# Every second pair of gate and side tiles of a ConvFFN made with seven half-size products instead of eight

## The chip, the cores and the metric

The kernel runs on one core of one Trainium2 chip. The metric is the device time of one execution in microseconds (us). TensorE multiplies, VectorE and ScalarE work on tiles in SBUF and PSUM, SyncE issues the loads of weights.

## What is computed

Two layers of a streaming encoder work on 512 tokens of 1024 features in float32. Layer 0 has a Mamba-2 mixer, layer 1 a short gated convolution; each is followed by a gated ConvFFN, and RMSNorms stand before and after each block. The change lies in the ConvFFN alone:

```python
FFN_HIDDEN = 2816
FFN_CONV_W = 3

def conv_ffn(h, w_up, conv_w, conv_b, w_down):
    up = h @ w_up
    gate = causal_dwconv(up[..., :FFN_HIDDEN], conv_w, conv_b)
    val = up[..., FFN_HIDDEN:]
    return (jax.nn.silu(gate) * val) @ w_down

x = x + rms_norm(f, ffn_post_g[i])        # f is what conv_ffn gives, for each layer i
```

## The kernel before

Activations are held with features on the 128 partitions and the 512 tokens in a row. A float32 product is made of three passes of TensorE: every operand is split in a high part (a copy in the type fp32r, made by ScalarE) and a low part (original minus high part, made by VectorE), and `three` multiplies high by high, low by high and high by low. A **unit** is one 1024x128 column strip of a weight matrix. SyncE loads it into one of two raw buffers (`w_raw`), ScalarE writes `w_hi` (`splits_to` there, L362), VectorE writes `w_lo` (`splits_to` there, L592), each into one of five slots, and TensorE runs it in `unit`: eight feature tiles by three passes, 24 matmuls of 128x128 by 128x512 (L863 to L865) into one PSUM bank. The first two units of each stage are run as two halves of 256 tokens each (`half_unit`, 24 matmuls of 256 columns each), since they start while the norm before them is being finished.

The up stage of a layer takes the 22 hidden tiles t = 0 to 21 one after the other. Each has a gate unit and a side unit, in turn. Around them stands a fixed order of work, written by hand in `ffn_up`, once for ScalarE and once for VectorE:

- VectorE scales the gate bank by the norm's row into `cpad` (L807), makes the low part of a later unit (L592), adds the two early taps of the convolution (L794, twice), scales the side bank into `side` (L811), makes another low part (L592), multiplies gate by side into `gated` (L816), and makes the low part of that product, `hid_lo` (L799).
- ScalarE starts the convolution in `acc` (L549), makes a high part of a unit (L362), takes the SiLU (L553), makes another high part (L362), and makes `hid_hi` (L556).

All instructions of an engine run in the order written. The down stage (`project`) multiplies `hid_hi` and `hid_lo` with 22 units of the down matrix; every unit takes 24 matmuls of 512 columns. `enter` covers the joint of two stages, `boundary` is what ScalarE and VectorE do there. Semaphores order the engines: `w_lo_done` (a unit is ready), `unit_done` (a bank is complete), `gate_in` and `side_in` (a bank is free again).

Of the kernel before, what the change touches and what calls it, by code (L numbers as in the profile page):

```python
# [10 lines left out]
P = 128  # L11
# [4 lines left out]
def build(nc, x, mix_pre_g, mix_post_g, ffn_pre_g, ffn_post_g, ssd_w_in, ssd_conv_w, ssd_conv_b,  # L16
# [129 lines left out]
    SC_BANKS = (2, 3, 4, 5, 6, 7)  # L146
    AHEAD = 2
# [5 lines left out]
    with ctx:  # L153
# [27 lines left out]
        x_sums, r_pre_tok = col(3, C), col(3, C)  # L181
# [33 lines left out]
        with ExitStack() as rest:  # L215
# [10 lines left out]
            acc, gated, side = (sb(n, [P, T], stack=rest) for n in ("acc", "gated", "side"))  # L226
            hid_hi, hid_lo = sb("hid_hi", [P, FT, T], F32R, rest), sb("hid_lo", [P, FT, T], F32R, rest)
# [120 lines left out]
        def _(act):  # L348
# [3 lines left out]
            def splits_to(end):  # L352

                for u in range(split_at[0], min(end, U_END)):
                    act.wait_ge(raw_landed[u % 2], 16 * (u // 2 + 1))
                    if before(u) is not None:
                        act.wait_ge(unit_done, before(u) + 1)
                    elif u == U_OUT + 3:
# [117 lines left out]

            def post_sum(b, c, half):
                if 2 * c + half < 7:
                    act.wait_ge(proj_done, 7 * b.nth + 2 * c + half + 1)
                else:  # L480
                    act.wait_ge(unit_done, b.end)
# [33 lines left out]
            def boundary(b, first):  # L515
# [25 lines left out]
                nc.scalar.activation(r_pre_tok[:, b.nth, :], x_sums[:, b.nth, :], ACT.Sqrt, bias=eps[:], scale=1.0 / D).then_inc(pre_root, 1)  # L541
                splits_to(b.end + AHEAD + 2)
# [3 lines left out]
            def ffn_up(layer, t):  # L546
                u, n = U_UP[layer] + 2 * t, HID0[2 * layer] + t
                act.wait_ge(gate_in, n + 1)
                nc.scalar.activation(acc[:], cpad[:, CW - 1:CW - 1 + T], ACT.Identity, bias=one(col_ffn_b(layer, t)),  # L549
                                     scale=one(col_ffn_w(layer, CW - 1, t))).then_inc(acc_done, 1)  # L550
                splits_to(u + 4)
                act.wait_ge(tap_done, 2 * n + 2)
                nc.scalar.activation(acc[:], acc[:], ACT.Silu).then_inc(act_done, 1)  # L553
                splits_to(u + 5)
                act.wait_ge(gated_done, n + 1)
                nc.scalar.activation(hid_hi[:, t, :], gated[:], ACT.Copy).then_inc(hid_hi_done, 1)  # L556

            def sc_in(i):
# [6 lines left out]
                nc.scalar.activation(hid_hi[:, i, :], gated[:], ACT.Copy).then_inc(hid_hi_done, 1)  # L565
# [6 lines left out]
            for t in range(FT):  # L572
                ffn_up(0, t)
# [5 lines left out]
            for t in range(FT):  # L579
                ffn_up(1, t)  # L580
# [4 lines left out]
        def _(dve):  # L585
            split_at = [1]

            def splits_to(end):

                for u in range(split_at[0], min(end, U_END)):  # L590
                    dve.wait_ge(w_hi_done, u + 1)
                    nc.vector.tensor_tensor(w_lo[slot(u)][:], w_raw[:, u % 2, :], w_hi[slot(u)][:].bitcast(F32),  # L592
# [204 lines left out]
            def low_hidden(n, t):  # L797
                dve.wait_ge(hid_hi_done, n + 1)
                nc.vector.tensor_tensor(hid_lo[:, t, :], gated[:], hid_hi[:, t, :].bitcast(F32), ALU.subtract).then_inc(hid_lo_done, 1)  # L799

            sides = [0]

            def ffn_up(layer, t):
                u, n = U_UP[layer] + 2 * t, HID0[2 * layer] + t
                banks = [UP_BANKS[layer][2 * (t % 2) + half] for half in range(2)]
                dve.wait_ge(unit_done, u + 1)
                nc.vector.tensor_tensor(cpad[:, CW - 1:CW - 1 + T], bank[banks[0]][:], r_row[:, 0, :], ALU.mult).then_inc(gate_in, 1)  # L807
                splits_to(u + 4)
                taps(n, lambda tap: col_ffn_w(layer, tap, t))
                dve.wait_ge(unit_done, u + 2)  # L810
                nc.vector.tensor_tensor(side[:], bank[banks[1]][:], r_row[:, 0, :], ALU.mult).then_inc(side_in, 1)  # L811
                sides[0] += 1
                splits_to(u + 5)
                dve.wait_ge(side_in, sides[0])
# [356 lines left out]
```

## Time and profile before

| | |
|---|---|
| median of 3 runs | 1339.2 us (1339.18 to 1339.48) |
| time of the profiled execution | 1340.12 us |
| its span from the first to the last instruction | 1338.4 us |
| TensorE busy in it | 1327.8 us, 99% |
| VectorE busy | 786.2 us, 59% |
| ScalarE busy | 570.9 us, 43% |
| mean granted clock of TensorE | 0.999 |

The busy time of an engine is the time in which at least one of its instructions ran. Matmuls overlap in the pipeline, so the rate of TensorE is read from the starts of matmuls that follow each other and not from their lengths. Instructions of VectorE and ScalarE overlap too, by a little under 0.1 us, where the second doesn't wait for anything.

### The profile page before, as it was taken

Reading aid. Unit: us, or ns where it says so; the run is one execution under the profiler, and the core shown is the slowest. Engines: PE = TensorE matmul, PEld = TensorE weight load, DVE = VectorE, ACT = ScalarE, POOL = GpSimd, SP = SyncE. Lnnn points to the kernel's source line nnn. Section 1 sums busy time; section 2 is a strip of 40 time slices with the busy share of each in tenths; the row PEclk is TensorE's granted clock in tenths of the full one; section 3 lists DMA queues with packets and bytes.
Section 4 is the critical chain, followed back from the end, with each engine's and each line's share of the span. In section 5 each row is a group of like instructions: output and inputs, shape, how many; then the busy total and the mean of one; then the engine's idle time right before and its main releaser. Section 6 shows DMA issues by size and latency. Waiting matters only on the chain.

```text
span 1338.4 us, 15750 instructions
## 1 busy us (share of the span) xinstructions
PE 1327.8 (99%) x6382; PEld 1109.5 (83%) x6382; DVE 786.2 (59%) x1140; ACT 570.9 (43%) x875; POOL 28.1 (2%) x30
## 2 busy tenths in 40 slices
PE   8999999999999999999999999999999999999998
PEld 6888888888888888888888888888888888888886
DVE  5888888888526666556632265445566666564223
ACT  6766665556315533333331262223554333333112
POOL 1000000000000000000000000000000000000000
PEclk9999999999999999999999999999999999999999
DMA  5533233442331333333343313334233333334331
GB/s 155 158 110 110 80 97 109 125 121 69 128 108 48 95 107 98 95 95 95 95 137 115 95 32 112 102 102 126 63 88 102 95 97 101 102 96 126 97 109 63
DMA packets 181772, 135.68 MB, mean 101 GB/s; under 512 B 5645, under 2 KB 169893, under 8 KB 180677
## 3 DMA queue, kind: packets, MB, share of 16 engines
q1 hardware_dynamic: 181653, 134.62, 33.5%
q8 instruction: 50, 0.82, 0.3%
q14 instruction: 21, 0.17, 0.0%
q10 hardware_dynamic: 48, 0.07, 0.0%
HBM read 132.51 MB, written 2.16 MB: 101 GB/s over the span
## 4 chain that ended last, share of the span: by engine, by line
PE 98%; ACT 1%; DMA 1%; DVE 0%; issue 0%; SPq 0%; DVEq 0%; ACTq 0%
PE bank L863 22%; PE bank L864 22%; PE bank L865 22%; PE bank L926 9%; PE bank L928 9%; PE bank L927 9%; PE bank L1065 1%; PE bank L1075 1%; PE bank L903 1%; PE bank L1055 1%; DMA x_tok<-in_x 1%; PE bank L1048 1%; PE bank L1040 0%; PE bank L1043 0%; PE bank L1001 0%; ACT mask L423 0%
## 5 line engine op out<-in xcount | busy, mean ns | idle before, releaser
L863 PE MATMUL bank<-h_hi,w_hi 128*128 128x512 f32 (+1 forms) x1328 | 509.0, 383 | 0.0
L865 PE MATMUL bank<-h_lo,w_hi 128*128 128x512 f32 (+1 forms) x1328 | 506.7, 382 | 0.0
L864 PE MATMUL bank<-h_hi,w_lo 128*128 128x512 f32 (+1 forms) x1328 | 506.5, 381 | 0.0
L592 DVE TENSOR_TENSOR w_lo<-w_raw,w_hi 128x1024 fp32r<-128x1024 f32 x227 | 285.1, 1258 | 324.2 <-ACT w_hi L362 324.2
L362 ACT ACTIVATE w_hi<-w_raw 128x1024 fp32r<-128x1024 f32 x227 | 237.1, 1051 | 196.3 <-PE bank L928 172.5
L865 PEld LDWEIGHTS bank<-h_lo,w_hi 128*128 128x128 f32 x1328 | 249.5, 188 | 48.2
L863 PEld LDWEIGHTS bank<-h_hi,w_hi 128*128 128x128 f32 x1328 | 249.6, 188 | 48.0
L864 PEld LDWEIGHTS bank<-h_hi,w_lo 128*128 128x128 f32 x1328 | 249.7, 188 | 47.6
L926 PE MATMUL bank<-w_hi,hid_hi 128*128 128x512 f32 x416 | 162.4, 390 | 0.0
L928 PE MATMUL bank<-w_hi,hid_lo 128*128 128x512 f32 x416 | 161.9, 389 | 0.0
L927 PE MATMUL bank<-w_lo,hid_hi 128*128 128x512 f32 x416 | 161.8, 389 | 0.0
L928 PEld LDWEIGHTS bank<-w_hi,hid_lo 128*128 128x128 f32 x416 | 78.1, 188 | 16.3
L926 PEld LDWEIGHTS bank<-w_hi,hid_hi 128*128 128x128 f32 x416 | 78.1, 188 | 16.0
L927 PEld LDWEIGHTS bank<-w_lo,hid_hi 128*128 128x128 f32 x416 | 78.1, 188 | 15.9
L794 DVE SCALAR_TENSOR_TENSOR acc<-cpad,par,acc 128x512 f32<-128x512 f32 x104 | 77.9, 749 | 3.6 <-ACT acc L549 1.8
L621 DVE SCALAR_TENSOR_TENSOR feat<-pad,par,feat 128x512 f32<-128x512 f32 x96 | 71.5, 751 | 13.7 <-ACT feat L397 11.4
L553 ACT ACTIVATE acc<-acc 128x512 f32<-128x512 f32 x44 | 27.8, 633 | 115.8 <-DVE acc L794 115.8
L549 ACT ACTIVATE acc<-cpad,par 128x512 f32<-128x512 f32 x44 | 35.9, 815 | 88.8 <-DVE cpad L807 88.8
L556 ACT ACTIVATE hid_hi<-gated 128x512 fp32r<-128x512 f32 x44 | 27.8, 632 | 83.3 <-DVE gated L816 83.3
L799 DVE TENSOR_TENSOR hid_lo<-gated,hid_hi 128x512 fp32r<-128x512 f32 x52 | 36.0, 692 | 36.4 <-ACT hid_hi L556 30.8
L926 PE MATMUL bank<-w_hi,y_hi 128*128 128x512 f32 x128 | 50.3, 393 | 0.0
L928 PE MATMUL bank<-w_hi,y_lo 128*128 128x512 f32 x128 | 49.9, 390 | 0.0
(145 smaller groups left out, 941.7 us busy)
## 6 DMA issues: line engine op xcount, KB each, us to landing
w_raw<-in_ffn_w_up SPq DMA_DIRECT2D x88, 512.0 KB, 3.8
w_raw<-in_ssd_w_in SPq DMA_DIRECT2D x48, 512.0 KB, 3.9
w_raw<-in_ffn_w_down SPq DMA_DIRECT2D x44, 512.0 KB, 3.5
w_raw<-in_sc_w_in SPq DMA_DIRECT2D x24, 512.0 KB, 3.7
acs_b<-acs_dram SPq DMA_DIRECT2D x8, 1024.0 KB, 6.2
w_raw<-in_ssd_w_out SPq DMA_DIRECT2D x16, 512.0 KB, 3.5
w_raw<-in_sc_w_out SPq DMA_DIRECT2D x8, 512.0 KB, 3.6
x_tok<-in_x SPq DMA_DIRECT2D x4, 512.0 KB, 5.4
```

Of the source, the lines that this page charges most:

```text
L362: nc.scalar.activation(w_hi[slot(u)][:], w_raw[:, u % 2, :], ACT.Copy).then_inc(w_hi_done, 1)
L549: nc.scalar.activation(acc[:], cpad[:, CW - 1:CW - 1 + T], ACT.Identity, bias=one(col_ffn_b(layer, t)), scale=one(col_ffn_w(layer, CW - 1, ...
L592: nc.vector.tensor_tensor(w_lo[slot(u)][:], w_raw[:, u % 2, :], w_hi[slot(u)][:].bitcast(F32), ALU.subtract).then_inc(w_lo_done, 1)
L621: nc.vector.scalar_tensor_tensor(out=feat[:, f, :], in0=pad[:, f % 2, tap:tap + T], scalar=one(col_ssd_w(tap, page_tile)), in1=feat[:, f, ...
L794: nc.vector.scalar_tensor_tensor(out=acc[:], in0=cpad[:, tap:tap + T], scalar=one(cols(tap)), in1=acc[:], op0=ALU.mult, op1=ALU.add).then_ ...
L799: nc.vector.tensor_tensor(hid_lo[:, t, :], gated[:], hid_hi[:, t, :].bitcast(F32), ALU.subtract).then_inc(hid_lo_done, 1)
L863: nc.tensor.matmul(dst, wh, xh, start=start, stop=False)
L864: nc.tensor.matmul(dst, wl, xh, start=False, stop=False)
L865: return nc.tensor.matmul(dst, wh, xl, start=False, stop=stop)
L926: nc.tensor.matmul(dst[:], in_hi[:, k, toks], hi, start=k == 0, stop=False)
L927: nc.tensor.matmul(dst[:], in_hi[:, k, toks], lo, start=False, stop=False)
L928: last = nc.tensor.matmul(dst[:], in_lo[:, k, toks], hi, start=False, stop=k == b.tiles - 1)
```

## The change

Hidden tiles 0 to 5 of each layer stay as they were. From tile 6 on every other tile (6, 8, ... 20, eight in each layer) gets its gate and side unit together: the two weight strips are seen as a matrix of 2x2 blocks (rows: gate and side; columns: features 0 to 511 and 512 to 1023), the activations as 2x2 blocks too (features by early and late 256 tokens), and the product is made by Winograd's form of Strassen's scheme with seven products of blocks. Each product is 12 matmuls of 256 columns, so such a pair takes 84 of them, where it took 48 of 512 columns. Tiles 7, 9, ... 21 remain two units of `unit`.

VectorE makes all sums of blocks. Once in each layer those of the activations (`block_sums`, eight instructions of 1024 elements a row, with four high and four low parts, `t_high` and `t_low`); in each pair four sums of weights (`weight_sums`), and five sums of products with 256 elements a row. A pair has four slots of split weights: A11 and A12 (the gate strip itself), S3 and S2 (in `s_two`), S4 and A22 (in the raw buffer of the side strip), and half a slot for S1. Its raw strips have two buffers of their own, `w_raw_b`.

Three more things are changed with it. The side tile isn't scaled by the norm's row any more: the norm behind the FFN divides by the token's size, and its epsilon is corrected by `q_up`. The product of gate and side is written to `hid` and is split into high and low part (`hid_high`, `hid_low`) mostly during the down stage, into a ring of ten tiles, `hs_hi` and `hs_lo`. And the order of work is written anew for both engines.

```diff
+    PLAIN = 6
+    FP = (FT - PLAIN) // 2
+    FAST = [U_UP[layer] + 2 * (PLAIN + 2 * i) + half for layer in range(DEPTH) for i in range(FP) for half in range(2)]
...
@@ VectorE @@
-                nc.vector.tensor_tensor(side[:], bank[banks[1]][:], r_row[:, 0, :], ALU.mult).then_inc(side_in, 1)
...
-                nc.vector.tensor_tensor(gated[:], side[:], acc[:], ALU.mult).then_inc(gated_done, 1)
-                low_hidden(n, t)
...
+            def last_sums(layer, i):
+
+                n = FP * layer + i
+                dve.wait_ge(copied, COPIES * n + COPY_P6)
+                dve.wait_ge(prod_done, PRODUCTS * (n + 1))
+                nc.vector.tensor_tensor(pu[:], p6[:], bank[pair_bank(layer, AT_P5)][:, 0:HALF_T], ALU.add).then_inc(summed_up, 1)
+                dve.wait_ge(summed_up, SUMS * n + SUM_U)
+                nc.vector.tensor_tensor(late, pu[:], bank[pair_bank(layer, AT_P3)][:, 0:HALF_T], ALU.add).then_inc(summed_up, 1)
+                dve.wait_ge(summed_up, SUMS * n + SUM_C12)
+                whole = cpad[:, CW - 1:CW - 1 + T]
+                nc.vector.tensor_tensor(whole, whole, r_row[:, 0, :], ALU.mult).then_inc(gate_in, 1)
+                nc.vector.tensor_tensor(side[:, HALF_T:], pu[:], p7[:], ALU.add).then_inc(summed_up, 1)
...
+                nc.vector.tensor_tensor(s_one[:], a21, a22, ALU.add).then_inc(s_made, 1)
+                nc.vector.tensor_tensor(s3, a11, a21, ALU.subtract).then_inc(s_made, 1)
+                dve.wait_ge(s_made, 4 * n + 1)
+                nc.vector.tensor_tensor(s2, s_one[:], a11, ALU.subtract).then_inc(s_made, 1)
+                dve.wait_ge(s_made, 4 * n + 3)
+                nc.vector.tensor_tensor(a21, a12, s2, ALU.subtract).then_inc(s_made, 1)
...
+            def ffn_up(layer):
+                for t in range(PLAIN):
+                    u, last, end = U_UP[layer] + 2 * t, t == PLAIN - 1, gate_of(FP * layer)
+                    gate_row(layer, t)
+                    if last:
+                        aa_low(layer, 0)
+                    else:
+                        splits_to(min(u + 4, end))
+                    gate_taps(layer, t)
+                    if not last:
+                        splits_to(min(u + 5, end))
+                    gate_single(layer, t)
+                    if t in (1, 2):
+                        block_sums(layer, t - 1)
+                    if t in (3, 4):
+                        t_low(layer, 2 * (t - 3))
+                        t_low(layer, 2 * (t - 3) + 1)
+                    if t == PLAIN - 2:
+                        weight_sums(layer, 0)
+                    if last:
+                        ss_low(layer, 0)
+                        sa_low(layer, 0)
+                        s1_low(layer, 0)
...
@@ ScalarE, where a pair begins @@
+                    act.wait_ge(prod_done, PRODUCTS * n + 1)
+                    if n:
+                        act.wait_ge(summed_up, SUMS * n)
+                    nc.scalar.copy(p1[:], bank[pair_bank(layer, AT_P1)][:, 0:HALF_T]).then_inc(copied, 1)
...
@@ TensorE @@
+            def up_pair(layer, i):
+                n = FP * layer + i
+                t_hi, t_lo = ([t_part(hs, k) for k in range(4)] for hs in (hs_hi, hs_lo))
+                pe.wait_ge(aa_lo_done, n + 1)
+                if n:
+                    pe.wait_ge(summed_up, SUMS * n)
+                block(layer, i, "A11 A12", 0, AT_P1, quarter(h_hi, 0, 0), quarter(h_lo, 0, 0), True, True)
+                block(layer, i, "A11 A12", 1, AT_P2, quarter(h_hi, 1, 0), quarter(h_lo, 1, 0), True, True)
+                pe.wait_ge(ss_lo_done, n + 1)
...
+                block(layer, i, "S3 S2", 0, AT_P7, t_hi[0], t_lo[0], True, True)
+                pe.wait_ge(copied, COPIES * n + COPY_P1)
+                block(layer, i, "S3 S2", 1, AT_P1, t_hi[1], t_lo[1], False, True)
...
+                for i in range(FP):
+                    up_pair(layer, i)
+                    single(PLAIN + 2 * i + 1, 0)
+                    single(PLAIN + 2 * i + 1, 1)
```

The order changes most on VectorE. Before, each hidden tile of the up stage was the following cycle on VectorE (here tile 1 of layer 0; `cpad` takes the gate, `side` the side bank, the `w_lo` are low parts of units to come):

```order
L807 TENSOR_TENSOR cpad<-bank0,r_row 128x512 [waits unit_done]
L592 TENSOR_TENSOR w_lo1<-w_raw,w_hi1 128x1024 [waits w_hi_done]
L794 SCALAR_TENSOR_TENSOR acc<-cpad,par,acc 128x512 [waits acc_done]
L794 SCALAR_TENSOR_TENSOR acc<-cpad,par,acc 128x512 [waits tap_done]
L811 TENSOR_TENSOR side<-bank1,r_row 128x512 [waits unit_done]
L592 TENSOR_TENSOR w_lo2<-w_raw,w_hi2 128x1024 [waits w_hi_done]
L816 TENSOR_TENSOR gated<-side,acc 128x512 [waits act_done,side_in]
L799 TENSOR_TENSOR hid_lo<-gated,hid_hi 128x512 [waits hid_hi_done]
```

Now tile 1, before the first pair, has no step for the side bank and no `hid_lo`, and ahead of tile 2 it has the first four sums of activation blocks:

```order
L1090 TENSOR_TENSOR cpad<-bank0,r_row 128x512 [waits tap_done,unit_done]
L780 TENSOR_TENSOR w_lo1<-w_raw,w_hi1 128x1024 [waits w_hi_done]
L982 SCALAR_TENSOR_TENSOR acc<-cpad,par,acc 128x512 [waits acc_done]
L982 SCALAR_TENSOR_TENSOR acc<-cpad,par,acc 128x512 [waits tap_done]
L780 TENSOR_TENSOR w_lo2<-w_raw,w_hi2 128x1024 [waits w_hi_done]
L1097 TENSOR_TENSOR hid<-bank1,acc 128x512 [waits act_done,unit_done]
L1046 TENSOR_TENSOR hid<-h_hi,h_lo 128x1024 x2
L1056 TENSOR_TENSOR hid<-hid 128x1024 [waits t_made]
L1046 TENSOR_TENSOR hid<-h_hi,h_lo 128x1024
```

The two following tiles are loaded in the same way, with four sums and with two low parts. Tile 4, the last but one before the first pair, ends with two more low parts and the four sums of the pair's weights, and the low part of A11 and A12 follows behind the gate of tile 5:

```order
L1097 TENSOR_TENSOR hid<-bank7,acc 128x512 [waits act_done,unit_done]
L1027 TENSOR_TENSOR hs_lo<-hid,hs_hi 128x1024 [waits t_hi_done] x2
L1078 TENSOR_TENSOR s_one<-w_raw_b 128x512 [waits raw_landed3,raw_landed2]
L1079 TENSOR_TENSOR s_two<-w_raw_b 128x512
L1081 TENSOR_TENSOR s_two<-s_one,w_raw_b 128x512 [waits s_made]
L1083 TENSOR_TENSOR w_raw_b<-w_raw_b,s_two 128x512 [waits s_made]
L1090 TENSOR_TENSOR cpad<-bank0,r_row 128x512 [waits tap_done,unit_done]
L1003 TENSOR_TENSOR w_lo3<-w_raw_b,w_hi3 128x1024 [waits aa_hi_done]
```

In the run of pairs, the second half of VectorE's cycle is this (S3 and S2, the pair's product `hid`, the gate of the single tile, S4 and A22, its taps, S1, and its `hid`); all three low parts of a next pair's weights stand in it:

```order
L982 SCALAR_TENSOR_TENSOR acc<-cpad,par,acc 128x512 [waits acc_done]
L982 SCALAR_TENSOR_TENSOR acc<-cpad,par,acc 128x512 [waits tap_done]
L1009 TENSOR_TENSOR w_lo1<-s_two,w_hi1 128x1024 [waits ss_hi_done]
L1104 TENSOR_TENSOR hid<-side,acc 128x512 [waits t_lo_done,act_done,summed_up]
L1090 TENSOR_TENSOR cpad<-bank0,r_row 128x512 [waits tap_done,unit_done]
L1016 TENSOR_TENSOR w_lo2<-w_raw_b,w_hi2 128x1024 [waits sa_hi_done]
L982 SCALAR_TENSOR_TENSOR acc<-cpad,par,acc 128x512 [waits acc_done]
L982 SCALAR_TENSOR_TENSOR acc<-cpad,par,acc 128x512 [waits tap_done]
L1022 TENSOR_TENSOR w_lo3<-s_one,w_hi3 128x512 [waits s1_hi_done]
L1097 TENSOR_TENSOR hid<-bank1,acc 128x512 [waits act_done,unit_done]
```

On ScalarE the copy of product P1 out of its bank, for which TensorE's fourth block waits, stands behind all of the previous tile's work:

```order
L646 ACTIVATE acc<-cpad,par 128x512 [waits gated_done,gate_in]
L669 ACTIVATE w_hi1<-w_raw_b 128x1024 [waits prod_done,s_made]
L651 ACTIVATE acc<-acc 128x512 [waits tap_done]
L675 ACTIVATE w_hi2<-s_one 128x512 [waits unit_done,s_made]
L720 COPY p1<-bank2 128x256 [waits summed_up,prod_done]
```

Before, ScalarE copied nothing out of PSUM in the up stage; its last instruction on a tile was `hid_hi`, for which TensorE waited only in the down stage.

## Rows read from the trace of the kernel before

**Rows 1.** The page: span, and busy time of two engines.

```profile
span 1338.4 us, 15750 instructions
PE 1327.8 (99%) x6382; PEld 1109.5 (83%) x6382; DVE 786.2 (59%) x1140; ACT 570.9 (43%) x875; POOL 28.1 (2%) x30
```

**Rows 2.** Windows, layer 0's up stage: PE, PEld, DVE, ACT, POOL busy, PEclk, DMA.

```profile
430.00:660.00 230.00, 230.00 (x1064) 192.53 (x1063) 141.46 (x188) 91.56 (x128) 0.00 (x0) 1.00 0.33 97
```

**Rows 3.** Timeline of TensorE (start, length): 512-column units' start and end, 256-column run.

```profile
429.04 0.28 PE L863 MATMUL bank<-h_hi,w_hi 128*128 128x256 f32 x1
...
432.40 0.29 PE L864 MATMUL bank<-h_hi,w_lo 128*128 128x256 f32 x1
...
441.84 0.47 PE L863 MATMUL bank<-h_hi,w_hi 128*128 128x512 f32 x1
...
670.43 0.39 PE L926 MATMUL bank<-w_hi,hid_hi 128*128 128x512 f32 x1
```

**Rows 4.** Groups by form: matmuls of 256 columns and loads of weights (busy, mean ns, idle).

```profile
L863 PE MATMUL bank<-h_hi,w_hi 128*128 128x256 f32 x96 | 27.6, 288 | 0.0
...
L863 PEld LDWEIGHTS bank<-h_hi,w_hi 128*128 128x128 f32 x1328 | 249.6, 188 | 48.0
```

**Rows 5.** Timeline of VectorE: hidden tile 1 of layer 0, with idle time before.

```profile
448.78 0.69 DVE L816 TENSOR_TENSOR gated<-side,acc 128x512 f32<-128x512 f32 x1
450.16 0.69 DVE L799 TENSOR_TENSOR hid_lo<-gated,hid_hi 128x512 fp32r<-128x512 f32 x1 [0.70 <-ACT hid_hi L556]
450.77 0.69 DVE L807 TENSOR_TENSOR cpad<-bank,r_row 128x512 f32<-128x512 f32 x1
453.29 1.22 DVE L592 TENSOR_TENSOR w_lo<-w_raw,w_hi 128x1024 fp32r<-128x1024 f32 x1 [1.83 <-ACT w_hi L362]
454.43 1.53 DVE L794 SCALAR_TENSOR_TENSOR acc<-cpad,par,acc 128x512 f32<-128x512 f32 x2
455.88 0.68 DVE L811 TENSOR_TENSOR side<-bank,r_row 128x512 f32<-128x512 f32 x1
457.61 1.23 DVE L592 TENSOR_TENSOR w_lo<-w_raw,w_hi 128x1024 fp32r<-128x1024 f32 x1 [1.05 <-ACT w_hi L362]
...
460.74 0.69 DVE L807 TENSOR_TENSOR cpad<-bank,r_row 128x512 f32<-128x512 f32 x1
```

**Rows 6.** Timeline of VectorE: gates of hidden tile 0 and of tile 5.

```profile
442.87 0.69 DVE L807 TENSOR_TENSOR cpad<-bank,r_row 128x512 f32<-128x512 f32 x1
...
491.11 0.69 DVE L807 TENSOR_TENSOR cpad<-bank,r_row 128x512 f32<-128x512 f32 x1 [0.36 <-PE bank L865]
```

**Rows 7.** Timeline of ScalarE: the same hidden tile 1.

```profile
451.49 0.81 ACT L549 ACTIVATE acc<-cpad,par 128x512 f32<-128x512 f32 x1 [1.36 <-DVE cpad L807]
452.21 1.04 ACT L362 ACTIVATE w_hi<-w_raw 128x1024 fp32r<-128x1024 f32 x1
456.00 0.63 ACT L553 ACTIVATE acc<-acc 128x512 f32<-128x512 f32 x1 [2.74 <-DVE acc L794]
456.53 1.04 ACT L362 ACTIVATE w_hi<-w_raw 128x1024 fp32r<-128x1024 f32 x1
```

**Rows 8.** Groups by form: 256-element instructions on VectorE and ScalarE.

```profile
L704 DVE TENSOR_TENSOR prev<-prev,bank 128x256 f32<-128x256 f32 x16 | 6.7, 420 | 0.6
...
L458 ACT COPY prev<-bank 128x256 f32<-128x256 f32 x8 | 3.0, 372 | 1.9 <-PE bank L1055 1.9
```

**Rows 9.** The page's DMA issues: KB each, median us to landing.

```profile
w_raw<-in_ffn_w_up SPq DMA_DIRECT2D x88, 512.0 KB, 3.8
...
x_tok<-in_x SPq DMA_DIRECT2D x4, 512.0 KB, 5.4
```

**Rows 10.** TensorE's last matmul, then windows (PEclk third from the end).

```profile
1332.45 0.39 PE L928 MATMUL bank<-w_hi,hid_lo 128*128 128x512 f32 x1
...
1336.00:1337.00 1.00, 0.00 (x0) 0.00 (x0) 0.00 (x0) 0.00 (x0) 0.00 (x0) 0.82 0.93 344
1337.00:1338.40 1.40, 0.00 (x0) 0.00 (x0) 0.00 (x0) 0.00 (x0) 0.00 (x0) 0.50 0.34 129
```

More of the change, by code:

```diff
@@ L146, in build, with pair_bank @@
     SC_BANKS = (2, 3, 4, 5, 6, 7)
+    PAIR_BANKS = [(2, 3, 4, 5, 6), (4, 5, 6, 7, 0)]
+    AT_P1, AT_P2, AT_P7, AT_P3, AT_P5 = range(5)
+    def pair_bank(layer, which):
+        return PAIR_BANKS[layer][which]
+    SUM_C11, SUM_C21, SUM_U, SUM_C12, SUM_C22 = range(1, 6)
+    COPY_P1, COPY_P7, COPY_P6 = range(1, 4)
+    SUMS, COPIES = 5, 3
+    HALF_T = T // 2
+    RING, FIRST = 10, 2
     AHEAD = 2
@@ new lines, in hid_high @@
+            def hid_high(layer, end):
+                for k in range(hid_at[0], min(end, FT)):
+                    act.wait_ge(gated_done, HID0[2 * layer] + k + 1)
+                    if k >= RING:
+                        act.wait_ge(unit_done, nth(U_DOWN[layer] + k - RING))
+                    elif k >= FIRST:
+                        act.wait_ge(prod_done, PRODUCTS * FP * (layer + 1))
+                    nc.scalar.activation(hs_hi[:, k % RING, :], hid[:, k, :], ACT.Copy).then_inc(hid_hi_done, 1)
+                    hid_at[0] = k + 1
@@ L564, in sc_in @@
                 act.wait_ge(gated_done, n + 1)
[L565 removed]
+                nc.scalar.activation(hs_hi[:, i, :], hid[:, i, :], ACT.Copy).then_inc(hid_hi_done, 1)
             splits_to(U_OUT + SLOTS)
@@ new lines, in low_hidden, with hid_low, gate_taps @@
+                nc.vector.tensor_tensor(hs_lo[:, at, :], tile, hs_hi[:, at, :].bitcast(F32), ALU.subtract).then_inc(hid_lo_done, 1)
+            sides, hid_at = [0], [0]
+            def hid_low(layer, end):
+                for k in range(hid_at[0], min(end, FT)):
+                    low_hidden(HID0[2 * layer] + k, k % RING, hid[:, k, :])
+                    hid_at[0] = k + 1
+            def gate_taps(layer, t):
+                taps(HID0[2 * layer] + t, lambda tap: col_ffn_w(layer, tap, t))
@@ L845, in _ @@
             clear_pad(2)
-            for t in range(FT):
-                ffn_up(0, t)
+            ffn_up(0)
             boundary(back[1])
@@ L855, in _ @@
             clear_pad(4)
-            for t in range(FT):
-                ffn_up(1, t)
+            ffn_up(1)
             boundary(back[3])
@@ L1129, in taken, with hid_taken, wait @@
                 return wait
+            def hid_taken(layer, tiles):
+                def wait():
+                    pe.wait_ge(summed_up, SUMS * FP * (layer + 1))
+                    pe.wait_ge(gated_done, HID0[2 * layer] + tiles)
+                return wait
             up(0)
-            project(back[1], hid_hi, hid_lo, hid_landed(HID0[0]), {2: taken(FT - 1, FT - 1), 3: taken(FT, FT)})
+            project(back[1], hs_hi, hs_lo, hid_landed(HID0[0]), {0: hid_taken(0, FT - 2), 3: hid_taken(0, FT)})
             enter(back[1], SC_BANKS)
```

397 lines of the change are left out of this document (320 added, 77 removed).

## The prediction

> **What bounds the kernel now.** I read the page first: TensorE is busy for 1327.8 of 1338.4 us, VectorE for 786.2 [rows 1]. So in the mean TensorE is the bound. The change lies in the two up stages, so I read that stage next: in 230 us TensorE is busy throughout at full clock, VectorE for 141.5 us [rows 2]. The timeline then gives TensorE's rate. From 441.84 to 670.43 us stand 42 units of 24 matmuls, 228.6 us, so a matmul of 512 columns takes 0.2268 us and a unit 5.44; in the run of half units 28 matmuls of 256 columns take 3.36 us, 0.120 each [rows 3]. TensorE never waits there.
>
> But VectorE is nearer to the bound than 61% busy says, since it stands in a chain with ScalarE. Where it has fallen behind (it begins at 442.87, while TensorE is already at work) it runs a hidden tile in 460.74 - 450.77 = 9.97 us [rows 5, 6], with no wait for TensorE in it: each low part waits for a high part, each high part for the gate or the taps [rows 5, 7]. TensorE takes 10.88. VectorE catches up by 0.9 us a tile and first waits for TensorE at tile 5 [rows 6]. That margin is what the change spends.
>
> **What TensorE saves.** Sixteen pairs go from 48 x 0.2268 = 10.88 us to 84 x 0.120 = 10.08. That is 0.80 us each, 6.4 a layer, 12.8 in all. The loads of weights (188 ns each) don't set this rate: a matmul of 256 columns started each 0.120 us with such a load ahead of it [rows 3, 4]. The rule in the Trainium skill (TensorE: Matmul & The Clock Gate, Back-to-back issue gap) is columns over 2.4 GHz plus about 2.5 ns. By it a pair would go from 10.4 to 9.2 us and all pairs save 19 us; the rows have a fixed part nearer to 13 ns, so I use them.
>
> **The run of pairs.** One cycle is a pair and a single tile; TensorE needs 10.08 + 10.88 = 20.96 us. I walk VectorE through the same cycle, from start to start of instructions. Low parts of 1024 elements take 1.14 us, instructions of 512 take 0.61, two taps 1.45 [rows 5]. The sums of 256 elements aren't in this stage; the nearest row is 0.42 long [rows 8], 0.33 with the overlap of 0.09 that the others show. In the cycle stand five low parts (5.70), nine instructions of 512 (four weight sums, S1's low part, the scaling of the pair's gate, the single gate, two products: 5.49), two pairs of taps (2.90) and five sums of 256 (1.65). That is 15.7 us of work.
>
> The waits come on top. Before S3 and S2: after the taps ScalarE makes the SiLU and then the high part; from the end of the taps' place (455.88) to the low part (457.61) 1.73 us, which before was partly filled with `side` [rows 5, 7]. Before S4 and A22: as in 450.77 to 453.29 less 0.61, 1.91. Before S1: SiLU and a high part of 512, 1.3. Before the pair's first tap: 0.6. Sums that need the one before them: three times 0.12. Together 6.0, a cycle of 21.7 us. TensorE isn't in this chain: it waits for it, since its fourth block needs the copy of P1, which ScalarE makes only behind the SiLU and the S1 part of the tile before. So the pair costs TensorE 0.73 us of waiting, seven times a layer: 5.1 us. Instead of 21.76 us for two tiles there are 21.7: the saving is eaten.
>
> **Before the first pair.** Tiles 0 to 5 are walked in the same way. A plain tile loses the wait for `hid_hi` and `hid_lo`: 1.99 us from `gated` to the next gate become 0.60, so 9.97 becomes 8.58, and tile 0 goes from 7.90 to 6.5 [rows 5, 6]. Added are four sums of 1024 behind tile 1 (4.7), four behind tile 2 (4.8), two low parts behind tile 3 (2.3), and behind tile 4, which has one low part of a unit less, two low parts and four weight sums. The gates then come at 442.9, 449.4, 462.6, 476.0, 486.9 and 498.5 us, the low part of A11 and A12 ends at 502.3. TensorE is through its ten units at 441.84 + 54.4 = 496.2. It waits 6.1 us. The start after it is no row here; its price lies between nothing and a load of weights, 0.19 [rows 4], and I take 0.15. Two blocks later (505.3) it waits for S3 and S2, ready at 506.8: 1.45 us. The strips of the second pair can be issued only when the first pair's S4 part is done (507.7), and VectorE needs both at 511.1. One load lands in 3.8 us; four issued together had a median of 5.4 [rows 9]. So this costs 0.4 to 2 us; I take 0.7 above the 0.73 of the run.
>
> **The rest.** In the down stage VectorE and ScalarE get `hid`'s parts, 0.61 and 0.63 us beside a low and a high part for each unit of 5.44 us: hidden, unless the last pair leaves the first tiles late; the walk has them ready some 2 us early. If that cover went, its cost would be those 2 us.
>
> **Sum.** A layer: -6.4 + 6.1 + 1.45 + 5.1 + 0.7 = +6.95 us. Two layers: +13.9. On the profiled execution's 1340.1 us (span 1338.4 [rows 1] and 1.7 around it) that is 1354.0; the median of the runs is 0.9 lower, so 1353.
>
> **Rivals.** (1) *VectorE later still*: TensorE's long wait lets its clock fall. At the end of the program, after the last matmul at 1332.45, the granted clock is 0.82 in 1336 to 1337 and 0.50 after [rows 10], so a wait of 6.1 us is near enough to that for the first pair to start at 1.2 GHz. With every matmul of it at 0.24 us, the sixth product would be there at 519.7, where VectorE wants it at 515.4: up to 4.3 us a layer, nothing if the clock is soon back, since the first blocks have slack. With slow loads too (1.3 more) it would be 1353 + 11 = 1364. The same page of the Trainium skill (HAM oscillation) warns of gaps between bursts of matmuls for this reason; the rows show the fall, none shows the return. Chance 0.22.
>
> (2) *VectorE keeps pace in the run*: if the waits in its cycle are 0.73 us shorter, only the start costs: -12.8 + 2 x 7.6 = +2.4, 1341.6. For it: the 256-element sums are guessed. Against it: all five together are 1.65 us, and the waits are read from rows. Chance 0.09.
>
> (3) *Faster*: TensorE alone bounds, VectorE's chain is short everywhere: -12.8, 1326.4. The mechanism is the place of the low parts: it decides from the point at which the two stalls and the run together cost under 6.4 us a layer instead of 13.3. That needs the walk of 59.4 us up to the first pair and the 21.7 of the cycle both about 5% too long, yet these durations reproduce the present tile. Chance 0.05.
>
> (4) *The blocks don't run at 0.120*: weight loads bound them, 84 x 0.188 = 15.8 us a pair, +79 in all, 1418. The rows speak against it; 0.02.
>
> The forecast itself has 0.62, with 1348 to 1358. The range for 8 in 10 goes from 1344 to 1363; most of rivals 2 to 4 and the upper end of 1 stay out. A measurement tells 0.2% (2.7 us) from no change. Faster by more: 0.05; within: 0.07; slower: 0.88.
>
> **What would show it.** In the profile after: a wait of TensorE of about 6 us once in each layer, on the low part at L1003, then 1.4 us on L1009; a wait of 0.7 us in each later pair, put down to ScalarE's copy `p1`; VectorE's cycle 21.7 us, with idle time only before low parts and taps; matmuls of 256 columns at 0.120. I am wrong if that cycle is 20.96 with VectorE waiting for TensorE, if the first stall is under 3 us, or if the granted clock falls and stays low.

## The result, and the profile after

| | before | after |
|---|---|---|
| median | 1339.33 us (1339.18 to 1339.48, 4 runs) | 1356.11 us (1355.72 to 1357.17, 4 runs) |
| time of the profiled execution | 1340.12 us | 1356.22 us |
| its span | 1338.4 us | 1354.5 us |
| mean granted clock | 0.999 | 0.993 |

The changed kernel is slower: ratio 1.0127, 95% interval 1.0109 to 1.0144. It lost 16.8 us in the medians and 16.1 us in the profiled executions, where 13.9 were forecast.

The page of the changed kernel: its span and busy times (engine, us, share, instructions), and the chain of work that ended last, which before was TensorE for 98%:

```profile
span 1354.5 us, 17374 instructions
PE 1326.2 (98%) x6958; PEld 1134.8 (84%) x6958; DVE 876.2 (65%) x1296; ACT 611.5 (45%) x965; POOL 28.1 (2%) x30
PE 71%; DVE 14%; ACT 7%; issue 6%; DMA 1%; DVEq 0%; SPq 0%; ACTq 0%
```

VectorE has 90 us more work than in [rows 1]. TensorE's busy time hardly fell, partly because some of its work now runs at a lower clock (below). What counts is the second list: VectorE and ScalarE now stand in the chain for over a fifth of the span. TensorE's waits by line (what it waited for: us in total, times, longest) say where:

```profile
PE bank L1212 <- DVE w_lo L1003: 11.5, 2, 5.8
PE bank L1212 <- ACT p L720: 7.5, 12, 2.2
```

The first line is the low part of A11 and A12 for the first pair, once in each layer. The second is ScalarE's copy of P1 for later pairs: five of the seven in layer 0 (the second, then the fifth to the eighth) and all seven in layer 1.

TensorE's timeline in the up stages (start, length, what; in brackets the idle time before it), which answers to [rows 3]; from 992.64 on it is layer 1:

```profile
429.41 0.28 PE L1212 MATMUL bank<-h_hi,w_hi 128*128 128x256 f32 x1
...
442.22 0.47 PE L1212 MATMUL bank<-h_hi,w_hi 128*128 128x512 f32 x1
...
502.67 0.58 PE L1212 MATMUL bank<-h_hi,w_hi 128*128 128x256 f32 x1 [5.75 <-DVE w_lo L1003]
503.04 0.42 PE L1213 MATMUL bank<-h_hi,w_lo 128*128 128x256 f32 x1
503.26 0.41 PE L1214 MATMUL bank<-h_lo,w_hi 128*128 128x256 f32 x1
...
506.21 0.28 PE L1213 MATMUL bank<-h_hi,w_lo 128*128 128x256 f32 x1
506.33 0.28 PE L1214 MATMUL bank<-h_lo,w_hi 128*128 128x256 f32 x1
...
507.04 0.28 PE L1214 MATMUL bank<-h_lo,w_hi 128*128 128x256 f32 x1
507.16 0.28 PE L1212 MATMUL bank<-hs_hi,w_hi 128*128 128x256 f32 x1
...
531.89 0.39 PE L1212 MATMUL bank<-hs_hi,w_hi 128*128 128x256 f32 x1 [2.15 <-ACT p L720]
...
678.67 0.39 PE L1276 MATMUL bank<-w_hi,hs_hi 128*128 128x512 f32 x1
...
992.64 0.47 PE L1212 MATMUL bank<-h_hi,w_hi 128*128 128x512 f32 x1
...
1082.47 0.39 PE L1212 MATMUL bank<-hs_hi,w_hi 128*128 128x256 f32 x1 [1.20 <-ACT p L720]
...
1229.16 0.39 PE L1276 MATMUL bank<-w_hi,hs_hi 128*128 128x512 f32 x1
```

The stage takes 678.67 - 442.22 = 236.45 us where it took 228.59: 7.86 more. In layer 1 it takes 1229.16 - 992.64 = 236.52 where it took 228.59 too (984.41 to 1213.00 in the trace of before): 7.93 more. Together that is 15.8 of the 16.1 us. The stage of layer 0 begins 0.38 later than the 441.84 of [rows 3], but the whole trace is that much later by then: the entry took 441.84 - 429.04 = 12.80 us before and takes 442.22 - 429.41 = 12.81 now.

After the wait of 5.75 the matmuls start every 0.21 to 0.22 us (503.04, 503.26), after 506.2 every 0.12. There is no pause ahead of 507.16, the first matmul with S3 and S2. Their low part (L1009, below) ends at 506.93, and the slow matmuls ahead of it lasted until then.

VectorE's timeline, where the first pair and a later one are prepared, which answers to [rows 5]:

```profile
498.88 0.68 DVE L1090 TENSOR_TENSOR cpad<-bank,r_row 128x512 f32<-128x512 f32 x1
501.39 1.23 DVE L1003 TENSOR_TENSOR w_lo<-w_raw_b,w_hi 128x1024 fp32r<-128x1024 f32 x1 [1.83 <-ACT w_hi L657]
505.70 1.23 DVE L1009 TENSOR_TENSOR w_lo<-s_two,w_hi 128x1024 fp32r<-128x1024 f32 x1 [0.18 <-ACT w_hi L663]
...
513.78 0.69 DVE L1078 TENSOR_TENSOR s_one<-w_raw_b 128x512 f32<-128x512 f32 x1 [2.39 <-DMA w_raw_b<-in_ffn_w_up]
...
525.21 0.68 DVE L1090 TENSOR_TENSOR cpad<-bank,r_row 128x512 f32<-128x512 f32 x1
527.72 1.23 DVE L1016 TENSOR_TENSOR w_lo<-w_raw_b,w_hi 128x1024 fp32r<-128x1024 f32 x1 [1.83 <-ACT w_hi L669]
...
531.61 0.69 DVE L1022 TENSOR_TENSOR w_lo<-s_one,w_hi 128x512 fp32r<-128x512 f32 x1 [1.22 <-ACT w_hi L675]
...
542.00 1.54 DVE L982 SCALAR_TENSOR_TENSOR acc<-cpad,par,acc 128x512 f32<-128x512 f32 x2 [0.56 <-ACT acc L646]
545.18 1.23 DVE L1009 TENSOR_TENSOR w_lo<-s_two,w_hi 128x1024 fp32r<-128x1024 f32 x1 [1.65 <-ACT w_hi L663]
546.93 0.69 DVE L1090 TENSOR_TENSOR cpad<-bank,r_row 128x512 f32<-128x512 f32 x1
```

From gate to gate the cycle is 546.93 - 525.21 = 21.72 us. Its idle time stands where the forecast put it, each time released by ScalarE and never by TensorE: 1.83, 1.22, 0.56 and 1.65 us. The gate of tile 5 is at 498.88 (walked: 498.5), the low part at L1003 ends at 502.6 (502.3); with the 0.38 by which this trace is later, both were walked right.

Windows of layer 0's stage (length, then busy time and count of PE, PEld, DVE, ACT and POOL; third from the end is TensorE's granted clock):

```profile
500.00:507.00 7.00, 4.33 (x23) 4.33 (x24) 4.63 (x6) 4.26 (x6) 0.00 (x0) 0.56 0.00 0
528.00:538.00 10.00, 7.85 (x53) 7.65 (x52) 8.71 (x13) 4.81 (x8) 0.00 (x0) 0.83 0.61 170
538.00:670.00 132.00, 130.38 (x814) 117.83 (x813) 96.59 (x137) 55.20 (x80) 0.00 (x0) 1.00 0.32 92
```

In layer 0 the clock is low twice, after either of the two longer waits, and full in the rest. In layer 1 it is low once: after the first wait, of 5.75 us again, 28 matmuls start 0.21 us apart, and the second pair's wait of 1.20 us is followed by none. Both stages take the same 236.5 us.

### The profile page after: what moved, and what is told of

It reads as the page before. It is cut to its first block, busy times and chain, and to the rows that moved or that the text cites. A ratio compares the mean times of both kernels' runs of the same rounds, so it can differ in the third digit from the quotient of the medians.

```text
span 1354.5 us, 17374 instructions
## 1 busy us (share of the span) xinstructions
PE 1326.2 (98%) x6958; PEld 1134.8 (84%) x6958; DVE 876.2 (65%) x1296; ACT 611.5 (45%) x965; POOL 28.1 (2%) x30
## 4 chain that ended last, share of the span: by engine, by line
PE 71%; DVE 14%; ACT 7%; issue 6%; DMA 1%; DVEq 0%; SPq 0%; ACTq 0%
PE bank L1212 13%; PE bank L1214 13%; PE bank L1213 12%; PE bank L1276 9%; PE bank L1278 9%; PE bank L1277 9%; DVE acc L982 4%; ACT w_hi L445 1%; DVE w_lo L1016 1%; DVE w_lo L780 1%; DVE w_lo L1003 1%; DVE cpad L1090 1%; DMA w_raw_b<-in_ffn_w_up 1%; PE bank L1415 1%; ACT w_hi L663 1%
## 5 line engine op out<-in xcount | busy, mean ns | idle before, releaser
L1212 PE MATMUL bank<-h_hi,w_hi 128*128 128x512 f32 (+1 forms) x1264 | 466.5, 369 | 11.5 <-DVE w_lo L1003 11.5
L1276 PE MATMUL bank<-w_hi,hs_hi 128*128 128x512 f32 x416 | 162.4, 390 | 0.0
L1278 PE MATMUL bank<-w_hi,hs_lo 128*128 128x512 f32 x416 | 161.9, 389 | 0.0
L1277 PE MATMUL bank<-w_lo,hs_hi 128*128 128x512 f32 x416 | 161.8, 389 | 0.0
L1278 PEld LDWEIGHTS bank<-w_hi,hs_lo 128*128 128x128 f32 x416 | 78.1, 188 | 16.2
L1276 PEld LDWEIGHTS bank<-w_hi,hs_hi 128*128 128x128 f32 x416 | 78.1, 188 | 16.1
L1277 PEld LDWEIGHTS bank<-w_lo,hs_hi 128*128 128x128 f32 x416 | 78.1, 188 | 16.0
L1212 PE MATMUL bank<-hs_hi,w_hi 128*128 128x256 f32 x256 | 74.1, 289 | 7.5 <-ACT p L720 7.5
L1213 PE MATMUL bank<-hs_hi,w_lo 128*128 128x256 f32 x256 | 72.7, 284 | 0.0
L1214 PE MATMUL bank<-hs_lo,w_hi 128*128 128x256 f32 x256 | 72.7, 284 | 0.0
L651 ACT ACTIVATE acc<-acc 128x512 f32<-128x512 f32 x44 | 27.8, 632 | 95.3 <-DVE acc L982 95.3
L1212 PEld LDWEIGHTS bank<-hs_hi,w_hi 128*128 128x128 f32 x256 | 49.6, 194 | 9.9 <-ACT p L720 9.9
```

The costliest lines, as they stand in the source:

```text
L1212: nc.tensor.matmul(dst, wh, xh, start=start, stop=False, **more)
L1213: nc.tensor.matmul(dst, wl, xh, start=False, stop=False, **more)
L1214: return nc.tensor.matmul(dst, wh, xl, start=False, stop=stop, **more)
L1276: nc.tensor.matmul(dst[:], x_hi, hi, start=k == 0, stop=False)
L1277: nc.tensor.matmul(dst[:], x_hi, lo, start=False, stop=False)
L1278: last = nc.tensor.matmul(dst[:], x_lo, hi, start=False, stop=k == b.tiles - 1)
```

## Experiments

All ratios are against the kernel before, run on the same chip. Differences in us are to the changed kernel's 1356.11, unless said otherwise. Where the length of a stage is given, it is read in the profiled execution from the first matmul of 512 columns to the first of the down stage, as above.

### Does VectorE's cycle with ScalarE bound the run of pairs, or TensorE?

`e1_sum_twice` makes one weight sum of each pair twice, which adds work to VectorE alone:

```diff
+                nc.vector.tensor_tensor(s3, a11, a21, ALU.subtract).then_inc(again, 1)
+                dve.wait_ge(again, n + 1)
                 nc.vector.tensor_tensor(s3, a11, a21, ALU.subtract).then_inc(s_made, 1)
```

> The sum S3 is made twice in every pair, the second after the first, so VectorE gets 0.61 + 0.12 us more in each of 16 pairs, and TensorE nothing. If the chain of VectorE and ScalarE bounds the up stage, all of it is seen: +11.5 us, 1367.6. If TensorE's rate or the copy of P1 bounds it and VectorE has slack, the time stays at 1356.

Measured: 1367.33 us, ratio 1.0205 (1.0190 to 1.0221), 11.2 us more. TensorE's waits in it:

```profile
PE bank L1215 <- ACT p L721: 17.5, 12, 3.2
PE bank L1215 <- DVE w_lo L1004: 13.0, 2, 6.5
```

Both waits of the changed kernel grew, from 7.5 to 17.5 and from 11.5 to 13.0: 11.5 us for 16 sums, 0.7 each. The two stages are 11.6 us longer. One instruction of VectorE per pair shows in full.

`e2_more_matmuls` does the opposite: four more matmuls of 256 columns in each pair (0.48 us of TensorE), two in either block with A11 and A12, whose sums are then started afresh by the block's own first matmul.

```diff
+                if part == "A11 A12":
+                    for _ in range(2):
+                        nc.tensor.matmul(dst, w_hi[at][:, late * HALF_D:late * HALF_D + P], x_hi[:, 0, :], start=True, stop=True)
```

> Two more matmuls of 256 columns stand ahead of each of the first two blocks of every pair (their output is written over), 4 x 0.120 = 0.48 us of TensorE in each of 16 pairs. If the chain of VectorE bounds, TensorE's wait in a pair shrinks from about 0.75 to 0.3 us and the time stays within 1 us of 1356. If TensorE bounds, +7.7 us, 1364.

Measured: 1355.67 us, ratio 1.0119 (1.0104 to 1.0134). 16 times 0.48 is 7.7 us of TensorE's work, and the time didn't move. The wait for the copy shrank instead:

```profile
PE bank L1212 <- ACT p L720: 1.3, 2, 0.8
```

So in the run of pairs TensorE has slack and VectorE has none. The saving is there and can't be seen. The clock fell once in each layer here, and the stages took 236.66 and 236.43 us, the changed kernel's 236.45 and 236.52.

### Is it the place of ScalarE's copy that costs?

The waits name ScalarE's copy of P1, so a rival is that the copy only stands too late in ScalarE's order. `e3_copy_early` makes it a high part earlier:

```diff
-                    act.wait_ge(prod_done, PRODUCTS * n + 1)
-                    if n:
-                        act.wait_ge(summed_up, SUMS * n)
-                    nc.scalar.copy(p1[:], bank[pair_bank(layer, AT_P1)][:, 0:HALF_T]).then_inc(copied, 1)
+                    if i == 0:
+                        copy_p1(layer, i)
...
                         sa_high(layer, i + 1)
+                        copy_p1(layer, i + 1)
                     gate_silu(layer, t + 1)
```

> ScalarE copies P1 of the next pair before the SiLU of the single tile, not behind it and S1's high part. If the place of this copy, for which TensorE waits by the profile, is the cause, the waits of 0.75 us in 14 pairs go: -10 us, 1346. If the cycle of VectorE with ScalarE is the cause, TensorE waits elsewhere for the same cycle of 21.7 us, and the time changes by under 2 us.

Measured: 1353.87 us, ratio 1.0105 (1.0090 to 1.0121), 2.2 us less. The waits for the copy in it:

```profile
PE bank L1218 <- ACT p L728: 5.8, 13, 1.0
```

The wait moved to the next copy (L728, of P7) and each later pair still lost 0.55 to 0.58 us. The 11.5 us before the first pairs are unchanged. The copy was where the lateness came out, not its main cause: 10 us would have gone by the one theory and under 2 by the other, and 2.2 went. What the 2.2 are wasn't isolated.

### Take the weight sums off VectorE

`e4_sums_pool` gives the four weight sums of each pair to GpSimd, which is idle in the stage. The code is the same with `pool` for `dve`, in a loop of GpSimd's own:

```diff
+                pool.tensor_tensor(s_one[:], a21, a22, ALU.add).then_inc(s_made, 1)
+                pool.tensor_tensor(s3, a11, a21, ALU.subtract).then_inc(s_made, 1)
...
-                nc.vector.tensor_tensor(s_one[:], a21, a22, ALU.add).then_inc(s_made, 1)
-                nc.vector.tensor_tensor(s3, a11, a21, ALU.subtract).then_inc(s_made, 1)
...
```

> The four sums of weights of each pair go from VectorE to GpSimd. VectorE's cycle loses 4 x 0.61 + 0.12 = 2.6 us and falls to about 19.2 us, under TensorE's 20.96, and TensorE's first wait falls from 5.9 to about 3.4 us. By the theory that VectorE's chain bounds: -17 us, 1339. If GpSimd's sums (1.2 to 1.45 us each by the rows of before) slow VectorE or come late, less is won, 1345 to 1356.

Measured: 1355.30 us, ratio 1.0117 (1.0100 to 1.0134). That is a miss of the main case, at the upper end of the other: 2.4 us of work left VectorE in each pair and the cycle stayed at 588.71 - 566.92 = 21.79 us. VectorE's timeline of this kernel in one pair, and GpSimd's in the same stretch:

```profile
577.16 2.32 DVE L1025 TENSOR_TENSOR w_lo<-w_raw_b,w_hi 128x1024 fp32r<-128x1024 f32 x1
579.40 0.41 DVE L1151 TENSOR_TENSOR side<-p,bank 128x256 f32<-128x256 f32 x1
579.74 0.42 DVE L1059 TENSOR_TENSOR pu<-p,bank 128x256 f32<-128x256 f32 x1
580.20 0.42 DVE L1061 TENSOR_TENSOR cpad<-pu,bank 128x256 f32<-128x256 f32 x1
580.65 1.78 DVE L1064 TENSOR_TENSOR cpad<-cpad,r_row 128x512 f32<-128x512 f32 x1
582.36 1.51 DVE L1065 TENSOR_TENSOR side<-pu,p 128x256 f32<-128x256 f32 x1
```

```profile
576.40 2.00 POOL L439 TENSOR_TENSOR s_one<-w_raw_b 128x512 f32<-128x512 f32 x1 [14.60 <-DMA w_raw_b<-in_ffn_w_up]
578.35 2.28 POOL L440 TENSOR_TENSOR s_two<-w_raw_b 128x512 f32<-128x512 f32 x1
```

While GpSimd sums, the low part takes 2.32 us (1.23 otherwise), the scaling 1.78 (0.69) and a sum of 256 elements 1.51 (0.42). The three that read a PSUM bank keep their 0.41 and 0.42. So these three instructions, whose two inputs both lie in SBUF, get 1.09 us longer each, and those with one input in PSUM don't. One with both inputs in SBUF that had begun before GpSimd's sum, a low part at 576.02, kept its 1.22. The three lengthenings are 3.3 us, more than the work taken away; the wait of 0.56 us ahead of the pair's taps is gone, and the cycle comes out as before. The Trainium skill (SBUF — State Buffer, SBUF: two separate sides) says that VectorE and GpSimd share a pair of ports under an exclusive lock, which an instruction of VectorE with two SBUF inputs takes part in against one of GpSimd that reads SBUF. The trace agrees in which of the six were longer; the page gives no price, and the rows show 1.09 us.

### The loads of the second pair

The sum had 0.7 us a layer for them. In the changed kernel both strips wait for S4's low part of the first pair (L1016). `e5_gate_load` lets the gate strip go as soon as A11 and A12's low part is made:

```diff
-                    sp.wait_ge(sa_lo_done if of_pairs else w_lo_done, count)
+                    gate = of_pairs and u in FAST[::2]
+                    sp.wait_ge(aa_lo_done if gate else sa_lo_done if of_pairs else w_lo_done, count)
```

> The gate strip of the next pair is loaded when A11 and A12 have their low part, not when S4 and A22 have it, about 5.5 us earlier. The side strip then lands alone. VectorE's wait for it in the second pair falls from 2.39 to about 0.5 us, so a layer ends 1.9 us earlier: -3.5 us, 1352.6. If that wait was hidden by TensorE's second stretch at half clock, no change, 1356.

Measured: 1352.03 us, ratio 1.0093 (1.0076 to 1.0110), 4.1 us less. The weight sums of the second pair, which began at 513.78, 71.6 us into the stage, begin here 70.3 us into it:

```profile
512.01 0.68 DVE L1079 TENSOR_TENSOR s_one<-w_raw_b 128x512 f32<-128x512 f32 x1
```

TensorE's waits for the copy become

```profile
PE bank L1213 <- ACT p L721: 5.4, 13, 0.4
```

The longest wait for the copy falls from 2.2 to 0.4 us, and the second fall of the clock is gone with it. The stages take 235.09 and 234.57 us, so the late strips had cost 1.36 us in layer 0 and 1.95 in layer 1, 3.3 in both. The rest of the 4.1 lies outside the stages.

### How many pairs, and what the rest of the edits cost

`e6_plain20` sets `PLAIN` to 20, so that each layer has one pair; all other edits stay (the order, `hid`, `q_up`). `e7_plain8` sets it to 8, so that VectorE has two more tiles to catch up.

> Only one pair in each layer (hidden tile 20), all other tiles plain; block sums and the new order stay. VectorE has fourteen tiles at 8.6 against 10.88 us to make up the block sums, so no wait is left: -1.6 us for the two pairs and +0.8 us for the entry, 1338 to 1340. If the other edits (block sums, the split of hid in the down stage, q_up) cost by themselves, over 1343.

> Pairs start at tile 8, seven in each layer. VectorE gains 2 x 2.3 us on TensorE before the first pair, so the wait there falls from 5.9 to 1.3 us, at the price of one pair's 0.8 us and less one cycle bound by VectorE. By the walk -9.7 us, 1346.5. If the first wait doesn't come from the work of tiles 0 to 5, no change but the lost pair: 1357.

Measured: `e6_plain20` 1338.27 us (10 runs), ratio 0.9993 (0.9984 to 1.0003), no wait of TensorE for the up stages' parts. With one pair a layer the kernel is as fast as before. Its two pairs should save 1.6 us, and it is 1.1 faster than the 1339.41 of before in the same round, a difference that isn't clear of the noise. By the medians the other edits cost some 0.5 us at most, and the 0.8 that the expectation gave to the entry isn't there. `e7_plain8` 1346.28 us, ratio 1.0053 (1.0038 to 1.0068): the wait for A11 and A12 before the first pair (L1003) is down from 11.5 to 1.7 us, and that of the run stays.

```profile
PE bank L1212 <- ACT p L720: 8.4, 10, 2.6
PE bank L1212 <- DVE w_lo L1009: 2.4, 2, 1.2
PE bank L1212 <- DVE w_lo L1003: 1.7, 2, 0.9
```

The line of L1009 is new: it is the wait for S3 and S2, 1.2 us in each layer. After so short a first wait the first blocks ran at the full rate of 0.12 us a matmul, and this wait shows.

`e8_all8` puts the three remedies on top of `PLAIN = 8`: the sums on GpSimd, the early copy and the early gate strip.

> Pairs from tile 8 on, the weight sums on GpSimd, the copy of P1 early, and the gate strip loaded early. TensorE should bound everywhere: before - 14 x 0.80 + about 0.8 for the entry: 1329. If seven pairs still wait anywhere for 0.7 us, 1339.

Measured: 1338.02 us (10 runs), ratio 0.9990 (0.9981 to 1.0000), 9 us above what was expected. Its trace has the same long instructions (a low part at 550.02 takes 2.31 us), but how much of the 9 us is theirs wasn't isolated. TensorE still waits for S3 and S2 before the first pair (2.4 us in both layers), for A11 and A12 (0.6), for the copy (1.4) and, at the start of the down stages, for a low part (2.0): 6.4 us together.

### Put the sums where VectorE waits anyway

If the chain is VectorE with ScalarE, work that is moved into the idle time ahead of a low part is free. `e9_filled` moves two instructions of each pair. The low part of A11 and A12 goes behind the taps of the pair, and the fourth weight sum goes behind the gate of the single tile, where VectorE waited 1.65 and 1.83 us:

```diff
                         weight_sums(layer, i + 1)
-                        aa_low(layer, i + 1)
...
                     gate_taps(layer, t)
                     if more:
+                        aa_low(layer, i + 1)
                         ss_low(layer, i + 1)
...
                     gate_row(layer, t + 1)
                     if more:
+                        last_weight_sum(layer, i + 1)
                         sa_low(layer, i + 1)
```

> In the run of pairs alone VectorE's low part of A11 and A12 moves behind the taps of the pair (1.14 us into the wait of 1.65 for S3 and S2), and the fourth weight sum behind the gate of the single tile (0.73 us into the wait of 1.83). No work is taken away. VectorE's cycle falls from 21.7 to 19.9 us, under TensorE's 20.96. If these exposed waits made the cycle, the waits in pairs 2 to 8 go: by the walk -12.9 us, 1343. If VectorE's work as such bounds, or GpSimd-like contention of some kind, no change, 1356.

`e10_spread` does the same ahead of the first pair alone. The eight sums of activations are made one at a time in the two waits of tiles 0 to 4, where they stood in two groups of four behind the tile, and the parts S3 and S2 of tile 5 are made ahead of its SiLU:

```diff
                     gate_row(layer, t)
+                    if 1 <= t <= 4:
+                        block_sum(layer, 2 * t - 1)
...
                     gate_taps(layer, t)
+                    if t <= 3:
+                        block_sum(layer, 2 * t)
+                    if last:
+                        ss_low(layer, 0)
...
-                    if t in (1, 2):
-                        block_sums(layer, t - 1)
```

> In tiles 0 to 5 alone the eight sums of activation blocks go one by one into VectorE's waits for ScalarE (after each gate and after the taps), and S3 and S2 are split before the SiLU of tile 5. No work is taken away. If the first wait comes from their place, it is gone (5.9 and 1.4 us a layer) and the run of pairs alone is left with 0.7 us a pair: by the walk -15.7 us, 1340. If it comes from their amount, 1354 to 1356.

`e11_both` has both, and `q_up` behind ScalarE's copy of the row at the entry.

> Both reorderings, and q_up behind the copy of the norm's row. TensorE should never wait in the up stages: before - 16 x 0.80 = 1339.4 - 12.8 = 1326.6, that is 29 us under the change. If some of the waits only move, 1332 to 1345.

| kernel | median | ratio (95%) | to the changed kernel |
|---|---|---|---|
| `e9_filled` | 1344.23 us | 1.0041 (1.0026 to 1.0056) | -11.9 us |
| `e10_spread` | 1340.02 us (10 runs) | 1.0006 (0.9997 to 1.0016) | -16.1 us |
| `e11_both` | 1328.29 us | 0.9918 (0.9903 to 0.9933) | -27.8 us |

No instruction was taken away in any of them. TensorE's waits in `e9_filled` (in its slowest execution, 1347.51 us), then in `e10_spread`:

```profile
PE bank L1217 <- DVE w_lo L1003: 11.5, 2, 5.7
PE bank L1217 <- ACT p L720: 2.1, 1, 2.1
```

```profile
PE bank L1207 <- ACT p L720: 7.7, 10, 2.3
```

Each removes its own wait and leaves the other's; the 2.1 us of `e9_filled` and the 2.3 of `e10_spread` are the wait of the second pair for its strips. `e11_both` has none of them, and beats both kernels by 11.0 and 27.8 us. Its stages take 222.94 and 223.06 us. VectorE's timeline in it, over one cycle:

```profile
577.55 0.69 DVE L1085 TENSOR_TENSOR cpad<-bank,r_row 128x512 f32<-128x512 f32 x1
578.15 0.68 DVE L1078 TENSOR_TENSOR w_raw_b<-w_raw_b,s_two 128x512 f32<-128x512 f32 x1
580.07 1.23 DVE L1016 TENSOR_TENSOR w_lo<-w_raw_b,w_hi 128x1024 fp32r<-128x1024 f32 x1 [1.23 <-ACT w_hi L669]
...
591.11 0.42 DVE L1037 TENSOR_TENSOR pu<-p,bank 128x256 f32<-128x256 f32 x1 [1.03 <-PE bank L1214]
...
598.52 0.68 DVE L1085 TENSOR_TENSOR cpad<-bank,r_row 128x512 f32<-128x512 f32 x1
```

The wait of 1.83 us ahead of L1016 is 1.23 now, with the fourth sum in it. The cycle is 598.52 - 577.55 = 20.97 us, TensorE's 20.96, and VectorE waits for TensorE (1.03 us).

## Why the prediction was right, point by point

**Direction and size.** Slower by 13.9 us was forecast, by 16.8 measured; 1356.1 lies in the forecast's own range. The other cases with a price of their own (1364, 1341.6, 1326.4, 1418) are out.

**TensorE's saving, -6.4 us a layer: right.** Where the clock is full the matmuls of 256 columns start 0.12 us apart, each with its load of weights ahead. The stages of `e11_both` are 5.6 and 5.5 us shorter than before, with one wait for the copy left in each that costs 0.6 to 0.7. The Trainium skill gives its 2.5 ns (TensorE: Matmul & The Clock Gate, Back-to-back issue gap) for an isolated matmul and not for a stream with loads; the prediction applies it to such a stream, but its sum goes by the rows.

**The first wait, 6.1 us: right.** It is 5.9 in each layer, over the 0.23 at which matmuls of 512 columns follow each other. `e10_spread` takes it away together with the next term's: 5.9 and 1.6 us a layer are 15.0, and its two stages (229.12 and 228.77 us) are 15.1 shorter.

**S3 and S2, 1.45 us: right in size, but it shows in another form.** At full clock the first two blocks would have ended at 502.67 + 24 x 0.12 = 505.55, and the low part was there at 506.93, so TensorE would have waited some 1.4 us. In the trace it didn't wait: 16 matmuls at the lower clock filled that time, and the third block began at 507.16, 1.6 us late. The sign that the prediction gives, a wait of 1.4 us on L1009, isn't there. In `e7_plain8`, where the first wait is short and the matmuls behind it start 0.12 us apart, it is: 1.2 us.

**The run, 0.73 us a pair: right.** The cycle is 21.72 us where 21.7 was walked. Where TensorE waits in two pairs that follow each other, their fourth blocks begin 21.65 to 21.68 us apart, 0.7 over the 20.96 of its own work. In layer 0 the third and the fourth pair had no wait, since TensorE was still making up the second stretch of slow matmuls. `e1_sum_twice` and `e2_more_matmuls` show that VectorE's cycle with ScalarE is the bound and TensorE's isn't, `e3_copy_early` that the copy named by the wait is little more than its last link.

**The strips of the second pair, 0.7 us a layer: mis-sized.** They were issued as forecast,

```profile
508.09 0.99 SPq L358 DMA_DIRECT2D w_raw_b<-in_ffn_w_up  x2
```

but VectorE could begin only at 513.78, 5.7 us after the issue. It waited 2.39 us for the second strip, where the term had 0.7. From the third block of the first pair (507.16) to the fourth of the second (531.89) TensorE needed 24.73 us where its work takes 22.40: 2.33 lost, and 0.7 of it is the run's. So the term measured 1.6 us, inside the 0.4 to 2 that the prediction allowed; `e5_gate_load` takes back 1.36 and 1.95.

The layer then comes to -6.4 + 5.9 + 1.6 + 2.3 for the second pair + 6 x 0.7 = 7.6, measured 7.86 and 7.93; 0.3 I can't assign.

**What the sum left out.** Nothing that shows. The entry takes 12.8 us in both kernels. `e11_both` moves `q_up` behind the copy of the row, and its entry takes the same (428.94 to 441.74). That the other edits cost next to nothing `e6_plain20` shows.

**Rival 1, the clock.** Its mechanism is there, its price isn't. In layer 0 the first 16 matmuls after the wait of 5.75 us started each 0.213 us, which is the lower level, 1.2 GHz. That took 1.5 us, nearly all of it time in which TensorE would have waited for S3 and S2. The wait of 2.3 us before 531.89 was followed by the same: matmuls each 0.213 us from 533.4 to 536.8, another 1.5 us. The next pairs then had no wait, since VectorE's cycle sets the time and TensorE had slack in it. Layer 1 tells the clock from the strips: there it was low for 28 matmuls after the first wait and did not fall a second time, `e2_more_matmuls` has one fall in each layer, and all four stages take 236.4 to 236.7 us. So beyond S3 and S2's time the clock cost nothing that can be measured here. With less slack it may: in `e5_gate_load`, without the late strips, the stage with some 28 slow matmuls took 235.09 us and the one with 15 took 234.57.

## What to carry to other kernels

When a change trades TensorE's work for that of another engine, the busy shares don't price it: walk the other engine's cycle with its waits for its partner, here VectorE with ScalarE, and compare that cycle (21.7) with TensorE's (20.96). Work that is added to such a chain can cost its full length in one place and nothing in another: the same instructions made the kernel 16.8 us slower behind the waits and 11.0 us faster inside them. And the engine or copy that a wait names can be just the last link; doubling one instruction and adding a few matmuls tells which chain is bound. Two layers that do the same work are an experiment for free: here they differed in the clock and not in the time.

## What the runs showed of the hardware that was not expected

- GpSimd was no free place for VectorE's sums: in the cycle shown, the three VectorE instructions with both inputs in SBUF that began beside one took 1.09 us longer each, and the same sums took GpSimd 1.3 to 2.3 us where VectorE takes 0.69.
- A wait of TensorE of only 2.3 us was followed by matmuls at 1.2 GHz (16 of them, each 0.213 us), and they began 1.5 us after TensorE had gone on, not at once. After the wait of 5.75 us they began with the first, 16 of them in layer 0 and 28 in layer 1 of the same execution. Nor does a wait's length alone decide: in `e7_plain8` 28 slow matmuls followed the wait of 2.49 us in layer 0 (at 548.10), and none that of 2.65 in layer 1 (at 1095.39).
- Of two strips issued at 508.1 and 508.5 the first was there after 3.9 us, as one load alone is (3.8, [rows 9]), the second only 5.3 us after its own issue.
